# Token-major residual stream and norms in an eight-sublayer transformer kernel, with x-stationary output products over 512 weight columns

## The reference

```python
# block 1 (layer 0: gMLP mixer; layer 1: differential attention)
for layer in range(2):
    y = mixer(rmsnorm(h, norm_g[layer, 0]))
    h = h + rmsnorm(y, norm_g[layer, 1])
    y = conv_ffn(rmsnorm(h, norm_g[layer, 2]))   # (gelu(g) * u) @ w_down, g, u = causal conv of x @ w_up
    h = h + rmsnorm(y, norm_g[layer, 3])
# block 2
x = x + 0.5 * swiglu(rms_norm(x, ffn1_norm))
u = rms_norm(x, mix_norm) @ w_in                 # latent attention (8 heads) and block attention (8 heads)
x = x + concat(mla(u), moba(u)) @ w_out
x = x + 0.5 * swiglu(rms_norm(x, ffn2_norm))
return rms_norm(x, final_norm)
```

## Time and profile before

| | |
|---|---|
| median of three runs | 1165.03 us |
| profiled execution, first to last instruction | 1165.7 us |
| TensorE busy | 1113.5 us (96%) |
| TensorE weight loads (beside the matmuls) | 1084.9 us (93%) |
| VectorE busy | 810.1 us (69%) |
| ScalarE busy | 621.9 us (53%) |
| GpSimd busy | 68.5 us (6%) |
| read from memory | 188.58 MB, 164 GB/s over the span |
| mean granted TensorE clock | 0.985 |

### The profile page before, as it was taken

One profiled execution on the slowest core, in us unless ns is written; L12 is line 12 of the kernel. 1 busy time (PEld: TensorE's weight loads), 2 busy tenths in 40 slices (PEclk: granted clock), 3 DMA queues, 4 the chain that ended last, 5 costly groups with the idle time before them and its releaser, 6 DMA issues.

```text
span 1165.7 us, 23900 instructions
## 1 busy us (share of the span) xinstructions
PE 1113.5 (96%) x8840; PEld 1084.9 (93%) x8840; DVE 810.1 (69%) x1245; ACT 621.9 (53%) x1048; POOL 68.5 (6%) x79
## 2 busy tenths in 40 slices
PE   6798999999899889999998999999999999999996
PEld 5698999999799889999998999999999999999995
DVE  5587887776858768877777755655766868656554
ACT  5455655555646656655555644444554656444442
POOL 0077000000200001000001000000000000000000
PEclk9899999999999999999999999999999999999998
DMA  9763565555353243655554465565552435565630
GB/s 335 151 227 113 167 212 180 180 180 180 106 181 129 91 163 99 212 180 193 180 180 146 147 191 186 172 190 178 160 165 92 152 113 171 184 194 165 193 111 36
DMA packets 54033, 191.91 MB, mean 165 GB/s; under 512 B 6504, under 2 KB 6920, under 8 KB 53984
## 3 DMA queue, kind: packets, MB, share of 16 engines
q1 hardware_dynamic: 52272, 187.96, 49.5%
q0 software_dynamic: 1088, 2.63, 1.4%
q10 hardware_dynamic: 624, 0.64, 0.2%
HBM read 188.58 MB, written 2.62 MB: 164 GB/s over the span
## 4 chain that ended last, share of the span: by engine, by line
PE 87%; DVE 6%; DMA 4%; ACT 2%; issue 1%; POOL 0%; SPq 0%; DVEq 0%; ACTq 0%; POOLq 0%
PE G L1127 18%; PE G L1128 18%; PE G L1129 18%; PE Y L1127 8%; PE Y L1129 8%; PE Y L1128 8%; DMA raw<-in_panels 4%; DVE w_low L666 1%; PE PB L1144 1%; PE Y L1185 1%; PE Y L1187 1%; PE Y L1186 1%; ACT w_high L349 1%; PE PB L1290 1%; DVE rbc L677 1%
## 5 line engine op out<-in xcount | busy, mean ns | idle before, releaser
L1127 PE MATMUL G<-x_high,w_high 128*128 128x256 f32 x1712 | 489.1, 286 | 8.8 <-DVE x_low L684 8.8
L1128 PE MATMUL G<-x_low,w_high 128*128 128x256 f32 x1712 | 485.8, 284 | 0.0
L1129 PE MATMUL G<-x_high,w_low 128*128 128x256 f32 x1712 | 485.7, 284 | 0.0
L666 DVE TENSOR_TENSOR w_low<-raw,w_high 128x1024 fp32r<-128x1024 f32 x352 | 428.1, 1225 | 57.3 <-ACT w_high L349 56.8
L349 ACT CAST w_high<-raw 128x1024 fp32r<-128x1024 f32 x352 | 363.3, 1042 | 94.6 <-PE G L1129 65.5
L1127 PEld LDWEIGHTS G<-x_high,w_high 128*128 128x128 f32 x1712 | 329.9, 193 | 11.1 <-issue 9.6
L1128 PEld LDWEIGHTS G<-x_low,w_high 128*128 128x128 f32 x1712 | 330.0, 193 | 0.2
L1129 PEld LDWEIGHTS G<-x_high,w_low 128*128 128x128 f32 x1712 | 330.0, 193 | 0.0
L1127 PE MATMUL Y<-a_high,w_high 128*128 128x256 f32 x896 | 255.5, 285 | 0.0
L1128 PE MATMUL Y<-a_low,w_high 128*128 128x256 f32 x896 | 254.2, 284 | 0.0
L1129 PE MATMUL Y<-a_high,w_low 128*128 128x256 f32 x896 | 254.1, 284 | 0.0
(11 more groups left out here) (201 smaller groups left out, 889.5 us busy)
## 6 DMA issues: line engine op xcount, KB each, us to landing
raw<-in_panels SPq DMA_DIRECT2D x352, 512.0 KB, 3.7
rel_rows<-qk POOLq DMA_DIRECT2D x1, 1536.0 KB, 34.9
h<-in_x SPq DMA_DIRECT2D x4, 256.0 KB, 10.1
bias<-rel_rows POOLq DMA_DIRECT2D x8, 128.0 KB, 4.4
out_y<-big SPq DMA_DIRECT2D x4, 256.0 KB, 2.0
big<-in_w_s SPq DMA_DIRECT2D x1, 512.0 KB, 12.5
wc<-in_b_s SPq DMA_DIRECT2D x1, 512.0 KB, 13.9
cst<-in_consts ACTq DMA_DIRECT2D x1, 320.5 KB, 5.5
```

The costliest lines, as they stand in the source:

```text
L666: v.tensor_tensor(WL[:, j, :], raw[:, j, :], WH[:, j, :].bitcast(F32), ALU.subtract).then_inc(lo, 1)
L1127: mm(out, WH[:, j, c:c + w], xh, start=first, stop=False, skip_group_check=skip)
L1128: mm(out, WH[:, j, c:c + w], xl, start=False, stop=False, skip_group_check=skip)
L1129: return mm(out, WL[:, j, c:c + w], xh, start=False, stop=last, skip_group_check=skip)
```

## The change

- `h` becomes token-major, [128 tokens, 2 token tiles, 1024]. The norms are applied: per token tile ScalarE squares a row with an accumulator, takes the root, VectorE takes the reciprocal and multiplies by it and by the gain, which now lies in a row (`gain_pre`, `gain_post`, loaded anew for each sublayer to all partitions by SyncE, 512 KB each). TensorE turns the normalised x (`turn_x`, 16 matmuls of 128 x 128 into `Y`), ScalarE and VectorE split it into `x_parts`. The sums by matmul, `rbc`, `token_rms` and the multiplications by `rbc` go.
- Output products are x-stationary (`rows`): for each token tile 6 matmuls of 512 weight columns, 12 a panel.
- The last five output panels of each sublayer form a `tail`; `y_done` tells that token tile 0 is complete, 6 matmuls before token tile 1. The down panels of a feed-forward's last five hidden tiles are moved to its end.
- 6 warming matmuls stand at a boundary instead of 28; the six in the second mixer go. First tiles wait for all of x. GpSimd no longer adds.
- `raw` has 5 slots, `w_high` and `w_low` 8; loops are unrolled; hidden tiles are read from `G` (4 banks) directly; the gMLP mixing stands behind the sixth instead of the fourth tile; in the last mixer output panels move from between the last heads into the tail.

```diff
-            def rows_into_y(n, j, xh, xl, first, last):
-                ready(n)
-                for k in range(KT):
-                    end = product(Y[:, k, :], j, k * P, P, xh, xl, first and k % 2 == 0, last, skip=True)
...
+            def rows(n, slot, t, first, last):
+                ready(n)
+                j = n % RING
+                xh, xl = AH[:, slot, tok(t)], AL[:, slot, tok(t)]
+                for x, w, start, stop in ((xh, WH, first, False), (xl, WH, False, False), (xh, WL, False, last)):
+                    for c in range(2):
+                        end = mm(Y[:, 2 * t + c, :], x, w[:, j, half(c)], start=start, stop=stop)
+                if t == 1:
+                    end.then_inc(used, 1)
+                return end
+            def turn_x(b, t):
+                for c in range(2):
+                    pe.wait_ge(xn_r, quarter(b, t, c))
+                    for j in range(4):
+                        last = nc.tensor.transpose(Y[:, 2 * t + c, j * P:(j + 1) * P],
+                                                   xn[:, t, (4 * c + j) * P:(4 * c + j + 1) * P], ident)
+                    last.then_inc(xt_r, 1)
+            def first_tiles(b, outs):
+                n = STARTS[b]
+                turn_x(b, 0)
+                turn_x(b, 1)
+                pe.wait_ge(xl_r, quarter(b, 1, 1))
+                for m in range(4):
+                    tile_out(n + m, outs[m])
...
+            def boundary(b, func):
+                base = STARTS[b]
+                if b in POST:
+                    y_rms(b, 0)
+                    upto(base + 4)
+                h_rms(b, 0)
+                if b in POST:
+                    y_rms(b, 1)
+                if b < 7:
+                    x_high(b, 0)
+                h_rms(b, 1)
+                if b < 7:
+                    preload(func)
+                    x_high(b, 1)
...
+            def boundary(b):
+                base = STARTS[b]
+                if b in POST:
+                    y_scale(b, 0)
+                    link(y_normed(b, 0, 0))
+                    link(y_normed(b, 0, 1))
+                    h_add(0, 0), h_add(0, 1)
+                    half_mean(b, 0)
+                    upto(base + 4)
+                    x_normed(b, 0)
+                    y_scale(b, 1)
+                    link(y_normed(b, 1, 0))
+                    x_low(b, 0, 0)
+                    link(y_normed(b, 1, 1))
+                    x_low(b, 0, 1)
+                    h_add(1, 0), h_add(1, 1)
+                elif b:
+                    h_plus_y(b, 0)
+                    half_mean(b, 0)
+                    x_normed(b, 0)
+                    if b < 7:
+                        x_low(b, 0, 0), x_low(b, 0, 1)
+                    h_plus_y(b, 1)
+                half_mean(b, 1)
+                x_normed(b, 1)
+                if b < 7:
+                    x_low(b, 1, 0), x_low(b, 1, 1)
```

More of the change, by code:

```diff
@@ L262, in _ @@
[L262 to L268 removed]
+            for n in range(RAWS, PANELS):
+                for b in range(1, 8):
+                    if n == STARTS[b - 1] + 20:
+                        gains(b)
+                load(n)
@@ L269, in _ @@
+            for t in range(TT):
+                for c in range(2):
+                    sp.wait_ge(out_r, 2 * t + c + 1)
+                    sp.dma_start(io["out"][tok(t), half(c)], xn[:, t, half(c)]).then_inc(out_sem, 16)
             sp.wait_ge(out_sem, 64)
@@ L458, in ffn @@
-                for f in range(2 + 2 * turns, NF):
-                    static(f)
+                    hidden(ph, base, f, (lambda c, c0=c0: par[:, c0 + c:c0 + c + 1]) if with_conv else None)
+                preload(ACT.Sqrt)
+                upto(base + 3 * NF + 3)
             def exps(a):
@@ L519, in _ @@
[L519 removed]
             gate_u(3)
[L521 to L522 removed]
+            for k in range(4, KT):
+                high_s(k)
+            upto(23)
             act.wait_ge(ang_r, 1)
@@ L663, in _, with upto @@
             link = linker(dve, dv)
-            def split(j):
-                v.tensor_tensor(WL[:, j, :], raw[:, j, :], WH[:, j, :].bitcast(F32), ALU.subtract).then_inc(lo, 1)
-            def splits(first, last):
-                for n in range(first, last + 1):
+            made = [0]
+            def upto(last):
+                for n in range(made[0], min(last, PANELS - 1) + 1):
                     dve.wait_ge(hi, n + 1)
-                    split(n % RING)
-            def stat(b, post):
-                k = stat_at(b, post)
-                dve.wait_ge(st_std, k + 1)
-                v.reciprocal(rbc[:], rbc[:]).then_inc(st_bc, 1)
-                dve.wait_ge(st_bc, k + 1)
@@ new lines, in hidden @@
+                last.then_inc(pr, 1)
+                if not conv:
+                    gap(2)
+                gap(1)
+                dve.wait_ge(hh, i + 1)
+                v.tensor_tensor(AL[:, slot, :], wc[:, pf, 1, 0:T], AH[:, slot, :].bitcast(F32), ALU.subtract)\
+                    .then_inc(hl, 1)
+            def ffn(ph, base, with_conv):
+                for f in range(NF):
+                    c0 = C_CONV + (ph * NF + f) * 8
+                    hidden(ph, base, f, (lambda c, c0=c0: par[:, c0 + c:c0 + c + 1]) if with_conv else None)
+                upto(base + 3 * NF + 3)
@@ L871, in _ @@
             last.then_inc(mv_s, 1)
-            splits(12, 13)
+            dve.wait_ge(rowsum_r, 1)
+            dve.wait_ge(par_in, 16)
+            for k in range(KT):
+                r = Y[:, k // 4, (k % 4) * P:(k % 4 + 1) * P]
+                last = v.scalar_tensor_tensor(out=off[:, k, :], in0=r, scalar=par[:, C_LNB + k:C_LNB + k + 1],
+                                              in1=bsrow[:, k * P:(k + 1) * P], op0=ALU.mult, op1=ALU.add)
+            last.then_inc(off_r, 1)
+            upto(13)
             dve.wait_ge(lnsd_r, 1)
@@ new lines, in tail, with part @@
+            def tail(end, slots, before=None):
+                before = before or {}
+                def part(i, t):
+                    if (i, t) in before:
+                        before[i, t]()
+                    return rows(end - 5 + i, slots[i], t, False, i == 4)
+                for i in range(5):
+                    first = part(i, 0)
+                    if i == 4:
+                        first.then_inc(y_done, 1)
+                    part(i, 1)
+            def first_tiles(b, outs):
[5 more added lines that the diff above has]
+                    tile_out(n + m, outs[m])
```

1021 lines of the change are left out of this document (474 added, 547 removed).

## The result

The changed kernel takes 1212.12 us (median of four runs, 1210.86 to 1213.30), the kernel before 1164.47 in the runs beside it: 1.041 times the time, with a 95% interval of 1.039 to 1.044. The forecast was 1199 with a range of 1176 to 1217: the sign and the main mechanism (the boundaries) held, the time is 13 us above, and one term, the hole in the first mixer, went the other way. A launch's time is some 2 us longer than its span (1212.71 for 1210.5 us here). By that the profiled execution of before was the slowest of its three runs (1167.54), not one 0.7 us above the median; so the profiles show a loss of 44.8 us where the medians show 47.7.

The account below looks back on a forecast made before the run. The prediction took TensorE, busy for 96% of the span, as the bound. Its nine terms summed to +34.5 us against the profiled 1165.7, so 1200.2; with the median 0.7 lower, 1199 us, range 1176 to 1217.

Parts of the forecast that it names:

- Term 1: 112 output panels: 12 matmuls of 512 columns replace 24 of 256, 2.72 us for 2.88 a panel; -17.9 us.
- Term 2: Seven sums of squares by matmul and three per-token scale turns leave TensorE's stream; -7.9 us.
- Term 3: Start: x must be normalised, turned and split before the first product; +8.5 us, between +4 and +12.
- Term 4: gMLP mixer: six tiles instead of four before the mixing remove the 8.33 us wait; -9.6 us, at worst 0.
- first mixer's hole stays: Rival: the gMLP mixer's wait remains, its gain being 0; 1209 us, 5%.
- Terms 5 and 6: Longer norm chains at sublayer boundaries: four with a post norm +31.1 us, two without +22.8 us.
- Term 7: Half clock behind all six boundary gaps, 1.9 us each; +8 us, between 0 and 12.
- Term 8: Last mixer: the last head pair's attention loses the output panels between its scores and turn; +3 us.
- Term 9: End: shorter time from the last matmul's start to the end of the span; -3.5 us.
- tile 0 hidden: Rival: at boundaries tile 0's chain runs under the last panels, leaving gaps of 9.4 or 6.8 us; 1158.5 us, 6%.

Follow-up runs that it names:

- sized warming: Changed kernel with warming matmuls at every boundary sized to the gaps (24 or 8 ahead of tile 0's turns, 20 between tiles, 5 behind): 1197.59 us, ratio 1.029.
- experiment 7: Changed kernel with the last mixer's fourth output panel back between the last two heads and a tail of four panels there: 1207.45 us, ratio 1.035.
- experiment 5: Changed kernel with token tile 0 of all five last output panels ahead of token tile 1, some splits moved later: 1196.36 us, ratio 1.028.
- experiment 1: Changed kernel with GpSimd's 1.5 MB relative-bias write moved whole behind the first feed-forward's fourth panel: 1209.93 us, ratio 1.038.

## Why the prediction was right, and where it was not

- **Term 1, output products (-17.9).** Right in kind, a little high: 14.5 us in the stages of before, and 14.5 in all in after. 256 columns start 0.120 us apart, and 512 columns 0.229 in this kernel's output panels, not the 0.227 of the earlier trace rows; that makes 2.75 us a panel in place of 2.72. The issue gaps of the Trainium skill ("TensorE: Matmul & The Clock Gate", Back-to-back issue gap), 109 and 216 ns, which the page gives for isolated matmuls, are met at neither width here, and the 3 us that they would have made of this term were too few. What I left out is that finished banks come later; in before that gives back 1.7 us.
- **Term 2, sums (-7.9).** Not tried alone. In the last feed-forward, at full clock in both kernels, before takes 190.88 us and the sized warming's 186.80; the 22 output panels are 2.9 of these 4.1 us, which leaves 1.2 for its sum of squares, where I had 0.87. That is an estimate.
- **Term 3, start (+8.5).** +6.3, inside its bounds.
- **Term 4, the gMLP hole (-9.6).** This is the step that failed. I read "VectorE L884" in the earlier trace rows as the layer norm's own length and moved the norm's due time. The wait was for VectorE, VectorE's was for ScalarE, and ScalarE's for a panel under the bias write (26.97 us to landing in before). The change left that write alone and gave the panels five landing slots in place of six; the hole grew from 8.3 to 13.2 us. Shown by the hole that moves with the write and by the 14.6 us that its pieces give back. With the pieces the time is 1197.5, close to the 1199 of a forecast that had counted on no hole. How much of the growth is the fifth slot was not tried. The rival "first mixer's hole stays" had it at 1209, which was the nearest number of all, though the hole did not stay as it was but grew.
- **Terms 5 and 6, boundaries (+31.1, +22.8).** 64.9 us at the four with a post norm for 66.6, and 23.7 at the two without for 25.6. Adding up an unseen chain from the prices of like operations was good to 1.1 us a gap. ScalarE's table load stands at the fourth gap from 663.56 to 664.84, the next activation starts at 664.86 and its copy then still waits 0.68 us for TensorE, so it costs nothing. The drain that the Trainium skill ("ScalarE: Activation LUTs", What ACT_TABLE_LOAD costs) adds, by my estimate 8 us here, does not show.
- **Term 7, clock (+8).** The six stretches sum to 21.84 us at half clock, 10.9 lost, for 11.4 forecast. The sized warming gives back 11.3 in the stages, and 4.6 more in the gaps, which I had not counted as clock.
- **Term 8, last mixer (+3).** Undersized: 5.7 us of the stage by experiment 7. I counted the idle time and not the half clock behind it.
- **Term 9, end (-3.5).** -3.8.
- **Rival "tile 0 hidden".** It did not come about: tile 0 is complete only 1.4 us ahead. Its floor of 9.4 and 6.8 us was low by about 1.0 and 0.4 us, by the estimates of experiment 5. Whether an order of work that hides tile 0 wholly would bring the change below the kernel before was not tried.

## What to carry to other kernels

Where a wait names an engine that does many things in a fixed order, follow the chain of waits back until it leaves the engines; here it ended at a transfer 25 us old, and six tiles in place of four between the value products and the mixing did not help. A norm that is applied token by token puts a chain of three engines into every boundary, and the last token tile's part of it stays however early the other tile is done: by estimate 7 to 10 us here, and 11 to 13 as long as the first tile's late steps stand ahead of it in one engine's order; with the sum beside the products and the additions bank by bank, the kernel before has 1.3 to 1.6 us at two of these places. An idle stretch costs TensorE twice, the wait and the half clock behind it; the second can be had back with warming matmuls, counted in microseconds and not in number.

## What had not been expected of the hardware

- One transfer of 1.5 MB, copied 128 times out of eight partitions on GpSimd's queue, brings the whole core's transfers down to 123 GB/s at 65% busy engines (experiment 1's kernel), and panels of 512 KB that land in 4.4 us need 25.75 (after) and 26.97 (before). On a hardware queue the longest wait is still 15.1 us.
- A piece of it of 192 KB takes 8.9 us, twice an eighth of the whole, and does no harm.
- The half clock behind a gap lasts between 2.55 and 4.69 us in the six cases of after, with no order by the gap's length (14.5 us of gap has the shortest, one of 11.9 the longest). With warming matmuls through the gap it does not occur.
